# Two reorderings in the first projection of a two-block kernel: the fourth heads' root on ScalarE, the second filter's spectrum on VectorE

## What is computed

```
hn = modulate(rms_norm(h, norm1_g[layer]), shift1, scale1)
proj = hn @ w_in[layer]
qa, ka, va, qb, kb, vb = jnp.split(proj, splits, axis=-1)
qa = rms_norm(split_heads(qa, N_HEADS_A, HEAD_DIM), q_norm_a[layer])
ka = rms_norm(split_heads(ka, N_HEADS_A, HEAD_DIM), k_norm_a[layer])
va = split_heads(va, N_HEADS_A, HEAD_DIM)
...
qb = rms_norm(qb, q_norm_b[layer])
kb = rms_norm(kb, k_norm_b[layer])
```

```
hf = hyena_filter_freqs(L, *filt)
z = x1 * long_conv(v, hf[:, 0], bias[0])
y = x2 * long_conv(z, hf[:, 1], bias[1])
```

## Time and profile before

| | us |
|---|---|
| median of 3 runs | 1711.52 (1711.48 to 1712.55) |
| the profiled execution | 1711.36 |
| its span in the trace | 1709.6 |
| TensorE busy | 1358.6 (79%) |
| VectorE busy | 361.4 (21%) |
| ScalarE busy | 214.3 (13%) |
| the first projection, units 0 to 11 | about 40 to 166 |

### The profile page before, as it was taken

The page is one execution under the profiler, slowest core; times in us unless marked ns, Lnnn a source line. Parts: engine busy times, 40 slices in busy tenths (PEclk is TensorE's granted clock), DMA queues, the critical chain, the costliest instruction groups (busy, mean ns, idle before and its releaser), DMA issues.

```text
span 1709.6 us, 17817 instructions
## 1 busy us (share of the span) xinstructions
PE 1358.6 (79%) x7592; PEld 790.7 (46%) x7592; DVE 361.4 (21%) x769; ACT 214.3 (13%) x411; POOL 37.3 (2%) x68
## 2 busy tenths in 40 slices
PE   5979999999999998998766566576767657766665
PEld 3756587888888787884222122132312212221221
DVE  3556643223030355722000000000000000000001
ACT  2322422122210332101000000000000000000001
POOL 1100000000000001100000000000000000000000
PEclk8989999999999999998887888878687887787888
DMA  9785939566553833646999999999999999999996
GB/s 360 191 190 181 325 136 303 180 207 222 190 176 125 271 112 109 241 161 266 428 428 426 428 428 428 427 426 428 428 428 427 429 427 427 427 429 428 427 428 255
DMA packets 109583, 545.15 MB, mean 319 GB/s; under 512 B 5635, under 2 KB 72996, under 8 KB 78724
## 3 DMA queue, kind: packets, MB, share of 16 engines
q1 hardware_dynamic: 106444, 537.94, 80.0%
q10 hardware_dynamic: 2008, 2.86, 0.5%
q0 software_dynamic: 1056, 3.22, 0.5%
HBM read 539.81 MB, written 4.19 MB: 318 GB/s over the span
## 4 chain that ended last, share of the span: by engine, by line
PE 54%; DMA 37%; DVE 6%; issue 1%; ACT 1%; SPq 0%; DVEq 0%
DMA ring<-in_exp_w_dram 14%; DMA arena<-in_exp_w_dram 14%; PE L L1529 12%; DMA tok<-in_exp_w_dram 7%; PE X L1956 6%; PE L L1754 6%; PE X L1944 4%; PE L L1722 4%; PE X L1982 3%; PE X L1693 2%; PE L L1993 2%; PE L L1869 2%; PE L L1663 2%; DMA ring<-in_w_ada_dram 2%; PE X L1474 1%
## 5 line engine op out<-in xcount | busy, mean ns | idle before, releaser
L1956 PE MATMUL X<-arena,HR 128*32 128x512 f32 x1040 | 165.6, 774 | 76.9 <-DMA arena<-in_exp_w_dram 66.7
L1529 PE MATMUL L<-tok,ring 128*128 128x256 f32 x960 | 214.6, 384 | 2.0 <-ACT tok L585 1.6
L1529 PEld LDWEIGHTS L<-tok,ring 128*128 128x128 f32 x960 | 183.5, 192 | 39.3 <-issue 14.5
L1956 PE MATMUL X<-ring,HR 128*32 128x512 f32 x816 | 131.5, 779 | 63.8 <-DMA ring<-in_exp_w_dram 57.7
L1956 PEld LDWEIGHTS X<-arena,HR 128*32 128x32 f32 x1040 | 34.2, 131 | 193.7 <-DMA arena<-in_exp_w_dram 108.3
L1982 PE MATMUL X<-arena,HI 128*32 128x512 f32 x512 | 81.7, 771 | 48.7 <-DMA arena<-in_exp_w_dram 44.4
L836 ACT ACTIVATE HR<-X 128x512 f32<-128x512 f32 x16 | 9.6, 597 | 856.4 <-PE X L1956 856.4
L1381 DVE TENSOR_TENSOR HR<-HR,X 128x512 f32<-128x512 f32 x16 | 11.0, 688 | 472.4 <-ACT HR L836 472.4
L1982 PE MATMUL X<-ring,HI 128*32 128x512 f32 x400 | 67.9, 812 | 44.4 <-DMA ring<-in_exp_w_dram 41.0
L1754 PE MATMUL L<-tok,ring 128*128 128x256 f32 x448 | 101.0, 384 | 0.4 <-ACT tok L691 0.4
L1956 PEld LDWEIGHTS X<-ring,HR 128*32 128x32 f32 x816 | 26.9, 130 | 155.6 <-DMA ring<-in_exp_w_dram 89.2
(11 more groups left out here) (361 smaller groups left out, 1289.3 us busy)
## 6 DMA issues: line engine op xcount, KB each, us to landing
arena<-in_exp_w_dram SPq DMA_DIRECT2D x97, 2048.0 KB, 45.5
ring<-in_exp_w_dram SPq DMA_DIRECT2D x76, 2048.0 KB, 45.6
tok<-in_exp_w_dram SPq DMA_DIRECT2D x19, 2048.0 KB, 46.2
ring<-in_w_in_dram SPq DMA_DIRECT2D x34, 1024.0 KB, 9.9
ring<-in_w_ada_dram SPq DMA_DIRECT2D x24, 1024.0 KB, 7.9
ring<-in_ada_w_dram SPq DMA_DIRECT2D x24, 1024.0 KB, 4.8
ring<-in_w_up_dram SPq DMA_DIRECT2D x22, 1024.0 KB, 5.9
ring<-in_w_down_dram SPq DMA_DIRECT2D x11, 1024.0 KB, 4.9
```

The source lines that it names most:

```text
L1529: last = MM(L[:, j % 4, m * T:m * T + T], w[:, k, m * P:m * P + P], src(k), start=(k == 0), stop=(k == KT - 1))
L1956: last = MM(X[CAP * j:CAP * j + CAP, w, :], xe[:, k, :], mslot(g, u)[:, j * 512:j * 512 + 512], start=(k == 0), stop=(k == KT - 1))
```

## The change

Three pieces of code move, and no operation is added or removed.

1. ScalarE's `root(3)` stood between the copies of units 4 and 5. It now stands behind the four copies of the context's transposes, that is, behind unit 5 and ahead of unit 6.
2. ScalarE's `spectra(i - 6)` stood behind the root of its iteration. It now stands ahead of it. In iteration 6 there is no root; in iteration 7 `spectra(1)` is now ahead of `root(4)`.
3. VectorE's `filter_halves(1)` stood behind the fifth reciprocal (u = 4). It now stands at the head of that iteration, ahead of the reciprocal. `filter_halves(0)` stays where it was.

```diff
             for i in range(12):
                 if i in (4, 5, 10, 11):
                     raw(i, None)
-                    if i == 4:
-                        root(3)
                 else:
                     raw(i, u)
+                    if i in (6, 7):
+                        spectra(i - 6)
                     if u >= 1 and u != 4:
                         root(u - 1)
                     u += 1
...
                         A(hc[:, 2 * n:2 * n + 2, :].rearrange("p a t -> p (a t)"), L[:, pos["cT"][n] % 4, :],
                           ACT.Copy).then_inc(S["lin_emptied_by_act"], 1)
-                if i in (6, 7):
-                    spectra(i - 6)
+                    root(3)
...
             for u in range(8):
+                if u == 4:
+                    filter_halves(1)
                 dve.wait_ge(S["qk_sum"], u + 1)
                 dve.wait_ge(S["qk_raw"], u + 1)
...
                 if u == 3:
                     scale(3)
-                if u in (3, 4):
-                    filter_halves(u - 3)
+                    filter_halves(0)
```

## The result

| | before | after |
|---|---|---|
| median, us | 1711.75 (1711.48 to 1712.55, 4 runs) | 1697.08 (1695.38 to 1698.26, 4 runs) |
| the profiled execution | 1711.36 | 1695.38 |
| its span | 1709.6 | 1693.6 |

The ratio is 0.9913, with a 95% interval from 0.9896 to 0.9930: 14.9 us faster, between 12 and 18. The forecast was 1697.6. A second set of five runs gave 1697.36 and a ratio of 0.9916 (0.9902 to 0.9929).

A forecast was written before the change was run, and what follows sets the result against it. The chain that ended last was 54% TensorE, 37% DMA (expert weights at the end) and 6% VectorE; gains ahead of the experts count in full. 10.91 + 2.89 = 13.80 us off 1711.36 gave 1697.6 us, range 1696.0 to 1700.6.

The forecast's parts named there:

- Part 1: Moving root(3) behind the transposes' copies lets unit 6 follow the transposes without a gap; unit 7 starts 10.91 us earlier.
- The term for unit 6's clock: Without a long gap ahead, unit 6 takes 7.10 us at full clock instead of 8.39: 1.29 us of part 1.
- Parts 2 and 3: Second spectrum's copy and halves go ahead of root(4) and the reciprocal of u = 4; unit 8 gains 2.89 us more.
- They work only together: Parts 2 and 3: ScalarE's copy must not wait for the reciprocal, and VectorE's halves must not stand behind it.
- The delay costed at nothing: The reciprocal of u = 4 and root(4) come later, until 126.5 us, but unit 8 covers them: no cost.
- 2.5 us to spare: Cover claimed between the end of root(4) at 126.5 us and the end of unit 8 at 129.06.
- The transfers: Weights for later units have 15 us and more of cover; the bias load, landing at 137, has thirteen.
- The sum reaches the end: The 13.80 us carry through attention and expert loads to the kernel's end; no listed TensorE wait there ends with a DMA.
- The second spectrum gives nothing: Rival: delayed reciprocal and root push work behind unit 8 back, losing the 2.89 us; 1700.5 us, chance 0.06.
- no change: Rival: weights, bias or expert stream keep their old times and the gain is given back; 1711.4 us, chance 0.04.
- Unit 6 still slow: Rival: half clock for another reason, or a table load, costs 1.3 us at unit 6; 1698.9 us, chance 0.07.
- The bias comes late: Rival: bias load, requested among weights, lands at 173.9 and delays VectorE's line 961 by 10.0 us; 1721.4 us, chance 0.03.

The follow-up runs named there:

- the experiments: Changed kernel with two or three further VectorE reciprocals between the second spectrum's halves and the reciprocal of u = 4: 1696.48 and 1698.14 us, against 1697.36.
- the late request: Changed kernel with the bias load requested two units later, behind the root of u = 6: 1701.08 us, ratio 0.9934.
- `root(3)` alone: Kernel before with only root(3) moved behind the copies of the transposes: 1703.01 us, ratio 0.9950.
- the later square: Changed kernel with ScalarE's square of the context input moved into the attention's fourth pair: 1697.27 us, against 1697.36 beside it.

## Why the prediction was right

- **Part 1, 10.91 us.** The trace shows 10.93. Its steps hold to a few hundredths once the 2.21 us are taken off: unit 6 foreseen at 93.39, and the transposes ahead of it end at 93.35; the first `HN` foreseen at 104.29, measured 104.27; unit 7 foreseen at 106.17, measured 106.15. The new small delay behind `root(3)` is there as well, a wait of 0.57 us against 0.29 in the second spectrum. The kernel with `root(3)` between the copies shows that the mechanism is the ring of banks. The term for unit 6's clock, 1.29 us, was one execution's: in the timeline of TensorE that unit took 8.60 us in the first profile of before, 8.90 in the second, and 7.07 after.
- **Parts 2 and 3, 2.89 us.** The trace shows 119.71 - 106.15 = 13.56 us from unit 7 to unit 8 instead of 16.47: 2.91. "They work only together" is wrong: ScalarE's order alone has 1.3 of it. Only VectorE's part needs the other, by the circle of waits named above. On the kernel before, the two parts are worth this 2.9 (2.2 measured); on top of part 1 they are worth more, 14.4 - 8.6 = 5.8 us by the ratios and 4.5 to 5.7 by the traces, since they also remove the gap in which the clock fell. The prediction has no term for this. For the sum of all parts none is needed, since the gap is gone; for part 1 alone its 10.91 would have been too much by 2.3 us.
- **The delay costed at nothing.** Right in its result, wrong in its size: "2.5 us to spare" was the time until ScalarE has its next copy to do, and not until TensorE needs one. The head sums of u = 6 come behind unit 9; the experiments give 9 us.
- **The transfers.** The bias was requested at 123.58 and took 13.6 us instead of 10.5, among the weights; it landed at 137.2 and was used at 147.81 (the DMA moved 352 to 397 GB/s from 124 to 136 us). The cover was 10.6 us, not thirteen. No wait of TensorE in the projection ended with a DMA.
- **The sum reaches the end.** 15.96 us at the expert load against 16.0 at the end: nothing is lost or won on the way in these two traces. That the median, 1697.08, lies 0.5 us from the forecast is closer than the method can claim: the runs of one kernel spread over some 3 us.
- **The rivals.** "The second spectrum gives nothing" and "no change" fell. "Unit 6 still slow" did not occur (7.07 us), and the Sqrt needed no table load: from 92 to 151 us ScalarE's timeline after the change has none. Where a load does stand, at 153.09 us for 1.28, the next exponential starts 0.01 us behind its end, so its price here is no more than the 1.3 us of that rival. "The bias comes late" was put to the test by the late request, and the mechanism is real.

## What to carry to other kernels

When an engine's in-order program holds both a slow answer and cheap copies that free buffers, put the copies first. What counts is the copy that frees the buffer needed next: with the four transposes' copies left behind the wait, 8.7 of the 9.1 us of idle time came back. That a single copy left behind would do the same was not run.

Ask of each gap not only how long it is but what the clock does behind it. Two edits can be worth more together than the sum of each alone, as here, where one of them removes a gap in which the clock can fall. A cover is measured to the step at which the bounding engine needs the result, not to the next thing that the delayed engine has to do.

## What the runs showed of the hardware

Whether TensorE's clock falls in a wait of 3.2 to 3.3 us is not settled by its length. In the second block TensorE waits 3.30 and 3.31 us for line 1198 in two executions of the same changed kernel, each time ahead of four transposes and one half unit. First profile:

```profile
658.04 0.72 PE L1767 MATMUL L<-sq,arena 128*128 128x128 f32 x4 [3.30 <-DVE arena L1198]
658.59 5.31 PE L1754 MATMUL L<-tok,ring 128*128 128x256 f32 x16
```

Second profile:

```profile
661.14 0.72 PE L1767 MATMUL L<-sq,arena 128*128 128x128 f32 x4 [3.31 <-DVE arena L1198]
661.70 3.62 PE L1754 MATMUL L<-tok,ring 128*128 128x256 f32 x16
```

The same sixteen matmuls took 5.31 us and 3.62. Over the fourteen traces of this case they took 3.62 us in three (the second profile of the changed kernel, the first of `root(3)` alone, the later square) and 4.5 to 5.3 in the other eleven, always behind a wait of 3.30 or 3.31 us. This 1.7 us, and the 2.7 at unit 0, are of the size of the 3 us over which the runs of the changed kernel spread; a difference of one or two us between two traces of this kernel is first to be looked for there. (The Trainium skill, page "TensorE: Matmul & The Clock Gate", section "What's actually happening", says that the gate works on windows which run freely and do not start with the kernel; by that rule such differences between executions are expected, and these traces agree.) In the waits of 8.7 and 9.1 us the clock fell in all four traces that have them.

A short wait is no safety either. Ahead of unit 0, in the second profile of the changed kernel, TensorE's timeline shows nothing longer than 1.62 us:

```profile
37.14 1.05 PE L1485 MATMUL X<-cols,HI 128*128 128x4 f32 x8 [0.73 <-ACT HI L573]
39.82 9.88 PE L1529 MATMUL L<-tok,ring 128*128 128x256 f32 x32 [1.62 <-ACT tok L585]
```

Yet the granted clock goes from 1.00 to 0.50 there (windows, in the order of the others):

```profile
36.00:38.00 2.00, 1.27 (x12) 0.86 (x8) 0.00 (x0) 0.60 (x1) 0.00 (x0) 1.00 1.10 348
...
39.00:41.00 2.00, 1.18 (x3) 1.03 (x4) 2.00 (x6) 1.84 (x5) 0.00 (x0) 0.50 1.04 389
```

The first profile had the same two waits (0.73 and 1.62 us) and kept 1.00. So the length of a single wait does not say here what the clock does.
